# A two-layer encoder trunk on one core: the conditioning dot products of the projection and FFN loops move from TensorE to VectorE

## The chip, the cores and the metric

The kernel runs on one core of a Trainium2 chip. Its time is the device time of one execution, in microseconds (us); of several runs the median is given.

## What is computed

Two layers act on x (256 tokens, width 2048). Before each sublayer x is normalized by rows and modulated by vectors that come from one conditioning vector c. Cut to what matters:

```python
cond = silu(c)                                   # (1, 2048)
for l in range(2):
    mod = (cond @ w_ada[l] + b_ada[l])[:, None]  # w_ada[l]: 2048 x 12288
    sh1, sc1, g1, sh2, sc2, g2 = split(mod, 6)
    z = (rms_norm(x) * (1 + sc1) + sh1) @ w_in[l]
    mix = concat(diff_attention(z), latent_attention(z), spatial_gating(z)) @ w_out[l]
    x = x + g1 * mix
    h = rms_norm(x) * (1 + sc2) + sh2
    a = causal_conv(h @ w_up[l])                 # 3 taps a channel, 2 x 5632 channels
    x = x + g2 * ((silu(a_gate) * a_val) @ w_down[l])
```

All is float32. `cond @ w_ada` reads 201 MB of weights for 24576 results; this is the part that the change touches.

## The kernel before

**Units.** The large products are cut into units of weights, 1 MB each (a raw tile of 128 x 2048). SyncE loads a unit into `raw` (four slots). ScalarE makes its high part `whi` (L1007, in `split_hi`), VectorE its low part `wlo` (L1358, in `split_lo`), each with two slots, and TensorE (L542) does 48 matmuls with a unit: two chunks of 24, each of three products (high by high, high by low, low by high) over eight k. ScalarE may start on unit U when TensorE has done with unit U-2.

**Blocks and rows.** Four units are one block, that is one turn of a loop. The program is a list of rows of blocks (`make_phases`), and for each row each engine has a loop of its own (the first block is written out ahead of the loop in some rows). In layer 0 the rows are: win 6 and win 2 blocks (projection), attention, wout 4, then three times up and down: up 8, down 4, up 8, down 4, up 6, down 4. Layer 1 is alike, with its wout cut into 2 and 2. The units of the third down have 36 matmuls in place of 48.

**The order on VectorE and ScalarE.** In the loop of a block VectorE splits units 2, 3, 4 and 5 counted from the block's first, so always one or two ahead of TensorE. After each split comes the epilogue of one accumulator bank: two taps of the convolution (L1651, L1653) in up, one update of `xT` (L1663) in wout and down. ScalarE does the same with its splits, the first tap (L1250) and, at the end of an up block, the silu (L1256). GpSimd multiplies the two halves of an up block and splits the product (L500, L504, L507; the function is `gated`).

**The conditioning.** Its products are cut into 96 groups of 256 columns. A group comes in four parts of 512 KB, which GpSimd loads into the two slots of `ada` (L487), each when `ada_used` says that the part two before it is done with. On TensorE `ada_part` runs four matmuls a part on 32 columns each, with `condr` (cond, copied to 32 columns), into `B_ADA`; ScalarE copies the group's sums to `ya` (`ada_copy`); `ada_turn` sums their rows and turns them by two matmuls into `B_MOD`; VectorE adds the bias (`mod_add`, L1375). The first 16 groups run in the prologue, 12 in the attention of each layer, and 56 in the other rows, one to a block: all blocks of layer 0, the 8 win blocks of layer 1 and the first 2 of its wout. There a part follows the first chunk of each unit, and the turn the last chunk of the block.

**GpSimd's queue in an up loop** is one line of work: turn i loads parts 0, 1 and 2 of group i, then runs `gated(i - 1)`, then loads part 3. The load of part 2 waits for part 0 of the same group to be used. ScalarE's first tap of block i waits for the product of `gated(i - 1)` (`a_ready`).

Of the kernel before, what the change touches and what calls it, by code (L numbers as in the profile page):

```python
# [28 lines left out]
ALU = mybir.AluOpType  # L29
# [155 lines left out]
def bass_trunk(nc, consts, x, c, positions, w_ada, b_ada, w_in, da_q_gain, da_k_gain, da_lq1, da_lk1,  # L185
# [4 lines left out]
    with ExitStack() as ctx:  # L190
# [67 lines left out]
        T, _ = place("T", 4 * S)  # L258
        ya, _ = place("ya", 256)
        stat, _ = place("stat", 2 * 16)  # L260
        sml, _ = place("sml", 64)
# [21 lines left out]
        unit_done, chunk0_done = sem("unit_done"), sem("chunk0_done")  # L283
        ada_used, mod_turned = sem("ada_used"), sem("mod_turned")
        sub_done, ring_full = sem("sub_done"), sem("ring_full")
# [254 lines left out]
        def _(pe):  # L540
# [54 lines left out]

            def ada_part(g, q, slot, buf, lap):
                if q == 0 and not (isinstance(g, int) and g == 0):

                    pe.wait_ge(ya_ready, g)
                pe.wait_ge(ada_loaded[slot], 16 * lap)  # L600
                for j in range(4):
                    k = 4 * q + j
                    i_ = mm(B_ADA[32 * j:32 * j + 32, 0:256], condr[:, k * 32:(k + 1) * 32],
                            buf[:, slot * 1024 + j * 256:slot * 1024 + (j + 1) * 256], q == 0, q == 3)
                i_.then_inc(ada_used, 1)

            def ada_part_later(g, q):

                ada_part(g, q, q % 2, ada, A_PRO // 2 + 2 * (g - A_PRO) + q // 2 + 1)

            def ada_turn(g):

                pe.wait_ge(ya_ready, g + 1)
                if not (isinstance(g, int) and g == 0):

                    pe.wait_ge(mod_ready, g)
                for v in range(2):
                    i_ = mm(B_MOD[:, v:v + 1], ya[:, v * P:(v + 1) * P], con[:, C_SEL:C_SEL + 1], True, True)
                i_.then_inc(mod_turned, 1)
# [43 lines left out]
            for g in range(A_PRO):  # L663
                for q in range(4):
                    ada_part(g, q, (4 * g + q) % 8, apro, g // 2 + 1)
                    if q == 2 and g >= 1:
                        ada_turn(g - 1)
# [6 lines left out]
            ada_turn(A_PRO - 1)  # L674

            class Fill:


                def __init__(self, g):
                    self.g, self.calls = g, 0  # L680

                def __call__(self):
                    v = self.calls
                    self.calls += 1
                    if v < 10:
                        for q in range(2):
                            ada_part_later(self.g + v // 2, 2 * (v % 2) + q)
                    if v % 2 == 0 and v >= 2:
                        ada_turn(self.g + v // 2 - 1)

# [175 lines left out]

            def heads(l, g):
# [12 lines left out]

                for i in range(15):
                    if i < 12:
                        score(l, i)
                    if i in (4, 6, 8):
                        ms_rows(l, J_O, con[:, C_ROW1:C_ROW1 + 11], 1, only=(i - 4) // 2)
                    if i == 10:
                        spread(0)
                        spread(1)
                    if i == 11:
                        spread(2)  # L890
                    if 2 <= i <= 13:
                        turn_probabilities(l, i - 2)

                    if i < 2 * A_HEADS:
                        for q in range(2):
                            ada_part_later(g + i // 2, 2 * (i % 2) + q)
                    if i % 2 == 0 and i >= 2:
                        ada_turn(g + i // 2 - 1)
                    if 2 <= i <= 13:
                        values(l, i - 2)  # L900
# [22 lines left out]
            for l in range(L):  # L923
# [3 lines left out]
                for row in phases[l]:  # L927
                    kind, p, first, n, u0, b0, g0 = row
                    if kind == "small":
                        attention_inputs(l, u0, b0, Fill(g0))  # L930
                        heads(l, g0 + A_FILL)
                        continue
# [17 lines left out]
                    def body(i, waits):  # L950
                        for b2 in range(2):
# [4 lines left out]
                            for s in range(2):  # L956
                                v = 2 * b2 + s

                                def after_chunk(c_):
                                    if g0 is None:  # L960
                                        return

                                    if c_ == 0:
                                        ada_part_later(g0 + i, v)
                                    elif v == 3:
                                        ada_turn(g0 + i)

# [5 lines left out]
                    if begins and not (kind == "up" and p > 0):  # L973
                        body(0, input_ready)
                        start = 1
                    if start < n:
                        with pe.Fori(start, n) as i:
                            body(i, None)


# [14 lines left out]
        def _(act):  # L995
# [212 lines left out]
            for l in range(L):  # L1208
# [3 lines left out]
                for row in phases[l]:  # L1212
# [10 lines left out]
                    def body(i, ending=False):  # L1223
                        pb = sum(PASS_BLOCKS[:p])
                        pair = l * (FFC // 4) + pb + first + i
                        for b2 in range(2):
                            for c_ in range(2):
                                v = 2 * b2 + 2 + c_
                                if not (ending and b2 == 1):

                                    act.wait_ge(unit_done, d0 + 4 * i + v - 1)
                                    split_hi((u0 + v) % 4, (u0 + v) // 4 + i)
                                if v == 4 and g0 is not None:
                                    ada_copy(g0 + i)
                                if kind not in ("win", "up"):
# [42 lines left out]
        def _(dve):  # L1278
# [91 lines left out]
            def mod_add(g):  # L1370
# [3 lines left out]
                dst = mod[:, bass.ds(2 * at_, 2)]  # L1374
                tt(dst, B_MOD[:, 0:2], cols[:, bass.ds(COL_BADA + 2 * at_, 2)], ALU.add).then_inc(mod_ready, 1)  # L1375

            def t_free(idx):
# [240 lines left out]
            for l in range(L):  # L1618
                if l > 0:
                    trunk(l, J_N1, T_N1, 0)  # L1620
                for row in phases[l]:
# [13 lines left out]
                    def body(i, ending=False):  # L1635
                        n0 = order.n
                        order.plus = links * i
                        for b2 in range(2):
                            for c_ in range(2):
                                v = 2 * b2 + 2 + c_  # L1640
                                if not (ending and b2 == 1):
                                    split_lo(u0 + 4 * i + v, (u0 + v) % 4)
                                if kind == "win":
                                    continue
# [10 lines left out]
                                else:  # L1655
                                    if c_ == 0:
                                        dve.wait_ge(chunk0_done, b0 + 2 * i + b2 + 1)
                                    else:
# [5 lines left out]
                                        acc_free, 1)  # L1664
                        if g0 is not None:
                            mod_add(g0 + i)
                        assert order.n - n0 == links
# [6 lines left out]
                    m = n - ends  # L1674
                    if m > 0:
                        with dve.Fori(0, m) as i:
                            n0 = body(i)
                        order.n = n0 + links * m
                    if ends:
# [49 lines left out]
```

## Time and profile before

| | |
|---|---|
| median of 3 runs | 2923.38 us (2917.65 to 2926.26) |
| span of the profiled execution | 2919.7 us |
| TensorE busy | 2749.6 us, 94% |
| VectorE, ScalarE, GpSimd busy | 46%, 38%, 15% |
| share of TensorE in the chain that ended last | 85% |

The profile is of one execution. Its page gives busy times, the chain of waits that ended last, and groups of instructions; the trace behind it gives each instruction's start, length, and what ended the idle time ahead of it. TensorE's row is the one that a reader would look at first: in the loops it has no gap, and the other engines wait for it.

### The profile page before, as it was taken

To read this page: it belongs to the slowest core of one execution; us is meant where nothing else is said; L and a number is where in the kernel's file an instruction comes from. 1 tells how busy PE (TensorE), PEld (TensorE's weight loads), DVE (VectorE), ACT (ScalarE), POOL (GpSimd) and SP (SyncE) were. 2 spreads that over 40 slices of the span, in tenths; PEclk is the share of its full clock that TensorE was granted. 3 is DMA by queue.
4 is the path that set the end of the run, shared out by engine and by line. 5 is a ranking of instruction groups with operands and counts; after the bars stand their busy time and mean duration, and the time that the engine had idled before them with its cause. 6 is when DMAs were issued, how large, how long until landed. Compare 5 with 4: busy or idle time off the path is not lost.

```text
span 2919.7 us, 55413 instructions
## 1 busy us (share of the span) xinstructions
PE 2749.6 (94%) x22176; PEld 2440.2 (84%) x22176; DVE 1340.7 (46%) x1599; ACT 1119.0 (38%) x1295; POOL 431.8 (15%) x520
## 2 busy tenths in 40 slices
PE   6899887998999999999998998879989999999999
PEld 3499764697999999999987997546989999999998
DVE  1433336345444444444455333363455545554554
ACT  1333343225333333323334333432355534433443
POOL 4211111111221122212211111111001100110110
PEclk8699976799999999999999999877999999999999
DMA  9977653475777777777776775534535555555543
GB/s 321 333 238 237 191 193 119 143 238 173 237 238 238 238 237 240 236 242 233 236 226 194 238 239 185 195 123 159 188 130 172 186 178 183 186 174 187 176 159 126
DMA packets 443877, 595.89 MB, mean 204 GB/s; under 512 B 18124, under 2 KB 391936, under 8 KB 443520
## 3 DMA queue, kind: packets, MB, share of 16 engines
q1 hardware_dynamic: 388080, 392.45, 42.3%
q0 software_dynamic: 55296, 201.35, 20.5%
q8 instruction: 75, 1.23, 0.2%
q10 hardware_dynamic: 400, 0.65, 0.1%
q14 instruction: 26, 0.21, 0.0%
HBM read 592.30 MB, written 2.10 MB: 204 GB/s over the span
## 4 chain that ended last, share of the span: by engine, by line
PE 85%; DMA 7%; DVE 3%; ACT 2%; issue 2%; POOL 1%; POOLq 0%; ACTq 0%; DVEq 0%; SPq 0%
PE bank L542 84%; DMA ada<-in_w_ada_dram 4%; DMA apro<-in_w_ada_dram 1%; DMA raw<-in_w_in_dram 1%; ACT whi L1007 1%; DVE wlo L1358 0%; ACT sq L1074 0%; DVE T L1400 0%; DVE hlo L1405 0%; DMA rows<-in_b_ada_dram 0%; DVE r L1390 0%; PE bank L851 0%; PE bank L574 0%; POOL apro L481 0%; POOL yv L500 0%
## 5 line engine op out<-in xcount | busy, mean ns | idle before, releaser
L1358 DVE TENSOR_TENSOR wlo<-raw,whi 128x2048 fp32r<-128x2048 f32 x374 | 871.3, 2330 | 1223.2 <-ACT whi L1007 1223.2
L1007 ACT ACTIVATE whi<-raw 128x2048 fp32r<-128x2048 f32 (+2 forms) x386 | 725.4, 1881 | 1224.1 <-PE bank L542 1219.5
L542 PE MATMUL bank<-hhi,whi 128*128 128x256 f32 x3872 | 1121.2, 290 | 20.7 <-DVE hlo L1405 15.0
L542 PE MATMUL bank<-hlo,whi 128*128 128x256 f32 x3872 | 1097.7, 284 | 0.0
L542 PE MATMUL bank<-hhi,wlo 128*128 128x256 f32 x3872 | 1096.8, 283 | 0.0
L542 PEld LDWEIGHTS bank<-hhi,whi 128*128 128x128 f32 x3872 | 743.4, 192 | 88.5 <-issue 79.8
L542 PEld LDWEIGHTS bank<-hlo,whi 128*128 128x128 f32 x3872 | 745.3, 192 | 0.0
L542 PEld LDWEIGHTS bank<-hhi,wlo 128*128 128x128 f32 x3872 | 744.6, 192 | 0.0
L542 PE MATMUL bank<-mhi,whi 128*128 128x256 f32 x1920 | 555.5, 289 | 9.5 <-POOL mlo L507 8.4
L542 PE MATMUL bank<-mlo,whi 128*128 128x256 f32 x1920 | 544.9, 284 | 0.0
L542 PE MATMUL bank<-mhi,wlo 128*128 128x256 f32 x1920 | 544.5, 284 | 0.0
L487 POOL DMA_DIRECT2D ada<-in_w_ada_dram x320 | 241.0, 754 | 1598.7 <-PE bank L542 1548.5
L542 PEld LDWEIGHTS bank<-mhi,whi 128*128 128x128 f32 x1920 | 369.6, 192 | 41.7 <-issue 32.3
L542 PEld LDWEIGHTS bank<-mlo,whi 128*128 128x128 f32 x1920 | 370.2, 193 | 0.0
L542 PEld LDWEIGHTS bank<-mhi,wlo 128*128 128x128 f32 x1920 | 369.8, 193 | 0.0
L542 PE MATMUL bank<-ada,condr 128*32 128x256 f32 x2560 | 219.1, 423 | 48.1 <-DMA ada<-in_w_ada_dram 41.1
L500 POOL TENSOR_TENSOR yv<-yv,yg 128x512 f32<-128x512 f32 x44 | 56.9, 1293 | 734.9 <-DVE yv L1653 733.4
L542 PEld LDWEIGHTS bank<-ada,condr 128*32 128x32 f32 x2560 | 56.4, 113 | 115.1 <-DMA ada<-in_w_ada_dram 54.9
L542 PE MATMUL bank<-sq,con 128*128 128x256 f32 (+2 forms) x224 | 69.1, 446 | 39.1 <-ACT sq L1048 28.9
L1007 ACT ACTIVATE ya<-bank 128x256 f32<-128x256 f32 x96 | 36.7, 382 | 152.4 <-PE bank L542 152.4
L542 PEld LDWEIGHTS bank<-sq,con 128*128 128x128 f32 (+2 forms) x224 | 31.1, 164 | 73.0 <-issue 46.8
L542 PEld LDWEIGHTS bank<-con,ya 128*128 128x128 f32 x384 | 61.1, 225 | 26.2 <-issue 22.9
(170 smaller groups left out, 1668.1 us busy)
## 6 DMA issues: line engine op xcount, KB each, us to landing
raw<-in_ffn_w_up_dram SPq DMA_DIRECT2D x176, 1024.0 KB, 5.1
ada<-in_w_ada_dram POOLq DMA_DIRECT2D x320, 512.0 KB, 5.2
raw<-in_w_in_dram SPq DMA_DIRECT2D x64, 1024.0 KB, 7.0
raw<-in_ffn_w_down_dram SPq DMA_DIRECT2D x64, 1024.0 KB, 5.9
apro<-in_w_ada_dram POOLq DMA_DIRECT2D x64, 512.0 KB, 11.0
raw<-in_w_out_dram SPq DMA_DIRECT2D x32, 1024.0 KB, 6.7
raw<-in_ffn_w_down_dram SPq DMA_DIRECT2D x32, 768.0 KB, 4.9
raw<-in_mla_w_uq_dram SPq DMA_DIRECT2D x6, 768.0 KB, 5.7
```

Of the source, the lines that this page charges most:

```text
L487: pool.dma_start(slot_of(ada, q % 2), part_of(l, q, lg * 256)).then_inc(ada_loaded[q % 2], 16)
L500: pool.tensor_tensor(yv[:, 0:512], yv[:, 0:512], yg[:, 0:512], ALU.mult).then_inc(a_ready, 1)
L542: return pe.matmul(out_, lhsT, rhs, start=start, stop=stop, skip_group_check=True)
L1007: return act.activation(out_, in_, ACT.Copy)
L1358: tt(wlo[:, o:o + UNIT], raw[:, v4 * UNIT:(v4 + 1) * UNIT], whi[:, o:o + UNIT].bitcast(F32), ALU.subtract).then_inc(lo_ready, 1)
```

## The change

In the 56 blocks VectorE now forms the products: `dot_part` multiplies a part's four 128 x 256 tiles by one value of cond in each partition and adds them up in a tile `dot`. This takes four instructions a part, 16 a group, each of which waits for the one ahead of it. After a group TensorE only sums `dot` over its 128 rows, by two matmuls with a column of ones (`dot_turn`). `ada_copy` is gone there. The prologue and the attention are as before.

```diff
+            def dot_turn(g):
+
+                pe.wait_ge(ada_used, 4 * g + 4)
+                pe.wait_ge(mod_ready, g)
+                for v in range(2):
+                    i_ = mm(B_MOD[:, v:v + 1], dot[:, v * P:(v + 1) * P], one, True, True)
+                i_.then_inc(mod_turned, 1)
...
-                                    if c_ == 0:
-                                        ada_part_later(g0 + i, v)
-                                    elif v == 3:
-                                        ada_turn(g0 + i)
+                                    if c_ == 1 and v == 1 and not (isinstance(i, int) and i == 0):
+                                        dot_turn(g0 + i - 1)
...
+                    elif g0 is not None:
+                        body(0, None)
+                        start = 1
                     if start < n:
                         with pe.Fori(start, n) as i:
                             body(i, None)
+                    if g0 is not None:
+                        dot_turn(g0 + n - 1)
...
-                                if v == 4 and g0 is not None:
-                                    ada_copy(g0 + i)
...
+            def dot_part(g, q, done):
+
+
+                if q == 0:
+
+                    dve.wait_ge(mod_turned, g)
+                dve.wait_ge(ada_loaded[q % 2], 16 * (A_PRO // 2 + 2 * (g - A_PRO) + q // 2 + 1))
+                for j in range(4):
+                    k = 4 * q + j
+                    w = ada[:, (q % 2) * 1024 + j * 256:(q % 2) * 1024 + (j + 1) * 256]
+                    if k == 0:
+                        i_ = ts(dot[:, 0:256], w, sml[:, 32:33], None, ALU.mult)
+                    else:
+                        i_ = stt(dot[:, 0:256], w, sml[:, 32 + k:33 + k], dot[:, 0:256], ALU.mult, ALU.add)
+                    if j < 3:
+                        i_.then_inc(dot_step, 1)
+                        dve.wait_ge(dot_step, 12 * done + 3 * q + j + 1)
+                    else:
+                        i_.then_inc(ada_used, 1)
+                        dve.wait_ge(ada_used, 4 * g + q + 1)
...
                                 if not (ending and b2 == 1):
                                     split_lo(u0 + 4 * i + v, (u0 + v) % 4)
+                                if g0 is not None:
+                                    dot_part(g0 + i, 2 * b2 + c_, g0 + i - dots_on_pe)
+                                if v == 3 and g0 is not None and not (isinstance(i, int) and i == 0):
+                                    mod_add(g0 + i - 1)
...
-                        if g0 is not None:
-                            mod_add(g0 + i)
...
+                    if peeled:
+                        mod_add(g0 + n - 1)
```

On VectorE, the start of a block in an up loop, before; `hi_ready` is ScalarE's split, `tap_ready` its tap:

```order
L1358 TENSOR_TENSOR wlo<-raw,whi 128x2048 [waits hi_ready]
L1648 REGISTER_ALU
L1651 ISA [waits tap_ready]
L1651 SCALAR_TENSOR_TENSOR yg<-bank,cols,yg 128x255
L342 REGISTER_ALU
L1653 ISA [waits dve_order]
L1653 SCALAR_TENSOR_TENSOR yg<-bank,cols,yg 128x254
L1356 REGISTER_ALU
L1358 TENSOR_TENSOR wlo<-raw,whi 128x2048 [waits hi_ready]
```

and in the changed kernel:

```order
L1369 TENSOR_TENSOR wlo<-raw,whi 128x2048 [waits hi_ready]
L1393 REGISTER_ALU
L1394 ISA [waits mod_turned]
L1399 TENSOR_SCALAR dot<-ada,sml 128x256 [waits ada_loaded0]
L1404 ISA
L1401 SCALAR_TENSOR_TENSOR dot<-ada,sml,dot 128x256 [waits dot_step]
L1404 REGISTER_ALU
L1401 SCALAR_TENSOR_TENSOR dot<-ada,sml,dot 128x256 [waits dot_step]
L1404 REGISTER_ALU
L1401 SCALAR_TENSOR_TENSOR dot<-ada,sml,dot 128x256 [waits dot_step]
L1407 ISA
L1684 REGISTER_ALU [waits ada_used]
```

Four products now stand between the split and the taps that follow it. The waits on `dot_step` are carried by the products themselves, the wait for ScalarE's tap by an instruction of its own, as before.

On TensorE, the end of the first win row, where the loop is left, before:

```order
L542 MATMUL bank<-hhi,wlo 128x256
L613 REGISTER_ALU
L542 MATMUL bank<-con,ya 128x1 [waits mod_ready,ya_ready]
L542 MATMUL bank<-con,ya 128x1
L977 REGISTER_ALU
L977 COMPARE_AND_BRANCH
```

and in the changed kernel:

```order
L543 MATMUL bank<-hhi,wlo 128x256
L988 REGISTER_ALU
L988 COMPARE_AND_BRANCH
L543 MATMUL bank<-con,dot 128x1 [waits mod_ready,ada_used]
L543 MATMUL bank<-con,dot 128x1
L543 MATMUL bank<-hhi,whi 128x256 [waits acc_free,lo_ready]
```

The turn of a row's last group stands behind the loop and ahead of the next row's first unit; it waits for that group's four parts (`ada_used`).

On GpSimd the up loop is unchanged; in the changed kernel it reads:

```order
L487 REGISTER_ALU
L488 ISA [waits ada_used]
L488 DMA ada<-in_w_ada_dram 128x4x256
L500 ISA [waits silu_done]
L501 ISA
L501 TENSOR_TENSOR yv<-yv,yg 128x512 [waits acc_free]
L505 ISA [waits a_ready]
L505 COPY mhi<-yv 128x512
```

Nothing has moved here; what has moved is who raises `ada_used`: VectorE, after the split of unit 2, where it was TensorE in the middle of unit 0.

## Rows read from the trace of the kernel before

**Rows 1.** The page: its head, and the shares of the chain by engine.
```profile
span 2919.7 us, 55413 instructions
...
PE 85%; DMA 7%; DVE 3%; ACT 2%; issue 2%; POOL 1%; POOLq 0%; ACTq 0%; DVEq 0%; SPq 0%
```
**Rows 2.** Timeline, ScalarE, up block with a group: start, length, instruction, idle before.
```profile
1009.40 1.92 ACT L1007 ACTIVATE whi<-raw 128x2048 fp32r<-128x2048 f32 x1 [5.12 <-PE bank L542]
...
1025.82 0.39 ACT L1007 ACTIVATE ya<-bank 128x256 f32<-128x256 f32 x1 [1.56 <-PE bank L542]
...
1035.89 1.92 ACT L1007 ACTIVATE whi<-raw 128x2048 fp32r<-128x2048 f32 x1 [4.15 <-PE bank L542]
1038.96 0.57 ACT L1250 ACTIVATE yg<-bank,cols 128x256 f32<-128x256 f32 x1 [1.16 <-PE bank L542]
```
**Rows 3.** Timeline, ScalarE, one up block of layer 1, without a group.
```profile
2425.29 1.91 ACT L1007 ACTIVATE whi<-raw 128x2048 fp32r<-128x2048 f32 x1 [2.03 <-PE bank L542]
...
2448.33 1.91 ACT L1007 ACTIVATE whi<-raw 128x2048 fp32r<-128x2048 f32 x1 [2.03 <-PE bank L542]
```
**Rows 4.** Timeline, TensorE, on both sides of one part.
```profile
700.54 0.28 PE L542 MATMUL bank<-hhi,wlo 128*128 128x256 f32 x1
...
701.54 0.28 PE L542 MATMUL bank<-hlo,whi 128*128 128x256 f32 x1
```
**Rows 5.** Timeline, VectorE, a split and its two taps in an up block.
```profile
1011.35 2.29 DVE L1358 TENSOR_TENSOR wlo<-raw,whi 128x2048 fp32r<-128x2048 f32 x1 [4.29 <-ACT whi L1007]
1013.56 0.48 DVE L1651 SCALAR_TENSOR_TENSOR yg<-bank,cols,yg 128x255 f32<-128x255 f32 x1
1014.19 0.48 DVE L1653 SCALAR_TENSOR_TENSOR yg<-bank,cols,yg 128x254 f32<-128x254 f32 x1 [0.15 <-DVE yg L1651]
```
**Rows 6.** Timeline, VectorE, two instructions that follow on each other, and one alone.
```profile
88.75 0.56 DVE L1342 SCALAR_TENSOR_TENSOR dist<-dist 128x384 f32<-128x384 f32 x1
89.34 0.50 DVE L1344 TENSOR_SCALAR ang<-ang,con 128x256 f32<-128x256 f32 x1
...
682.29 0.48 DVE L1400 SCALAR_TENSOR_TENSOR T<-xT,sml,r 128x256 f32<-128x256 f32 x1
```
**Rows 7.** Timeline, GpSimd, in the block of rows 2.
```profile
1026.44 0.75 POOL L487 DMA_DIRECT2D ada<-in_w_ada_dram  x1 [5.72 <-PE bank L542]
1033.37 0.75 POOL L487 DMA_DIRECT2D ada<-in_w_ada_dram  x1 [6.18 <-PE bank L542]
1034.20 1.28 POOL L500 TENSOR_TENSOR yv<-yv,yg 128x512 f32<-128x512 f32 x1
```
**Rows 8.** Timeline at two row ends: layer 0's win, then its wout.
```profile
341.77 0.39 PE L542 MATMUL bank<-hhi,whi 128*128 128x256 f32 x1 [1.93 <-ACT z L1007]
...
664.39 0.50 PE L542 MATMUL bank<-con,ya 128*128 128x1 f32 x4
666.94 5.51 PE L542 MATMUL bank<-sq,con 128*128 128x256 f32 x17 [2.06 <-ACT sq L1074]
...
664.59 1.91 ACT L1007 ACTIVATE whi<-raw 128x2048 fp32r<-128x2048 f32 x1 [2.65 <-PE bank L542]
```
**Rows 9.** Timeline, ScalarE, one block of the third down of layer 0.
```profile
1498.38 1.91 ACT L1007 ACTIVATE whi<-raw 128x2048 fp32r<-128x2048 f32 x1 [3.16 <-PE bank L542]
...
1519.10 1.91 ACT L1007 ACTIVATE whi<-raw 128x2048 fp32r<-128x2048 f32 x1 [3.16 <-PE bank L542]
```
**Rows 10.** Timeline, ScalarE, third down of layer 1: two units on, TensorE waiting once.
```profile
2859.74 1.92 ACT L1007 ACTIVATE whi<-raw 128x2048 fp32r<-128x2048 f32 x1 [2.94 <-PE bank L542]
...
2868.82 1.92 ACT L1007 ACTIVATE whi<-raw 128x2048 fp32r<-128x2048 f32 x1 [2.93 <-PE bank L542]
```
**Rows 11.** TensorE after two gaps; stretches: us, busy, granted clock, DMA share, GB/s.
```profile
1487.90 0.45 PE L542 MATMUL bank<-mhi,whi 128*128 128x256 f32 x1 [1.86 <-POOL mlo L507]
...
1488.00:1491.00 3.00, 3.00 (x17) 0.51 0.53 168
...
2840.35 0.58 PE L542 MATMUL bank<-mhi,whi 128*128 128x256 f32 x1 [4.71 <-POOL mlo L507]
...
2840.00:2845.00 5.00, 4.65 (x22) 0.50 0.45 147
```

More of the change, by code:

```diff
@@ L259, in bass_trunk @@
         ya, _ = place("ya", 256)
+        dot, _ = place("dot", 256)
         stat, _ = place("stat", 2 * 16)
@@ L283, in bass_trunk @@
         unit_done, chunk0_done = sem("unit_done"), sem("chunk0_done")
-        ada_used, mod_turned = sem("ada_used"), sem("mod_turned")
+        ada_used, mod_turned, dot_step = sem("ada_used"), sem("mod_turned"), sem("dot_step")
         sub_done, ring_full = sem("sub_done"), sem("ring_full")
@@ L593, in turn_vectors, with ada_part @@
                     last.then_inc(pro_full, 1)
-            def ada_part(g, q, slot, buf, lap):
-                if q == 0 and not (isinstance(g, int) and g == 0):
-                    pe.wait_ge(ya_ready, g)
+            def ada_part(g, q, slot, buf, lap, copies):
+                if q == 0 and copies > 0:
+                    pe.wait_ge(ya_ready, copies)
                 pe.wait_ge(ada_loaded[slot], 16 * lap)
@@ L605, in ada_part, with ada_part_later, ada_turn @@
                 i_.then_inc(ada_used, 1)
[L607 to L613, printed above, removed]
+            def ada_part_later(g, q, copies):
+                ada_part(g, q, q % 2, ada, A_PRO // 2 + 2 * (g - A_PRO) + q // 2 + 1, copies)
+            def dot_turn(g):
[4 more added lines that the diff above has]
+                i_.then_inc(mod_turned, 1)
+            def ada_turn(g, copies):
+                pe.wait_ge(ya_ready, copies + 1)
                 if not (isinstance(g, int) and g == 0):
@@ L664, in _ @@
                 for q in range(4):
-                    ada_part(g, q, (4 * g + q) % 8, apro, g // 2 + 1)
+                    ada_part(g, q, (4 * g + q) % 8, apro, g // 2 + 1, g)
                     if q == 2 and g >= 1:
-                        ada_turn(g - 1)
+                        ada_turn(g - 1, g - 1)
                 if g == 2:
@@ L673, in _, with __init__ @@
                     turn_vectors()
-            ada_turn(A_PRO - 1)
+            ada_turn(A_PRO - 1, A_PRO - 1)
             class Fill:
-                def __init__(self, g):
-                    self.g, self.calls = g, 0
+                def __init__(self, g, copies):
+                    self.g, self.copies, self.calls = g, copies, 0
                 def __call__(self):
@@ L686, in __call__ @@
                         for q in range(2):
-                            ada_part_later(self.g + v // 2, 2 * (v % 2) + q)
+                            ada_part_later(self.g + v // 2, 2 * (v % 2) + q, self.copies + v // 2)
                     if v % 2 == 0 and v >= 2:
-                        ada_turn(self.g + v // 2 - 1)
+                        ada_turn(self.g + v // 2 - 1, self.copies + v // 2 - 1)
             def ring(l, e, b0):
@@ L865, in values, with heads @@
                     o_full, 1)
-            def heads(l, g):
+            def heads(l, g, copies):
                 def spread(v):
@@ L895, in heads @@
                         for q in range(2):
-                            ada_part_later(g + i // 2, 2 * (i % 2) + q)
+                            ada_part_later(g + i // 2, 2 * (i % 2) + q, copies + i // 2)
                     if i % 2 == 0 and i >= 2:
-                        ada_turn(g + i // 2 - 1)
+                        ada_turn(g + i // 2 - 1, copies + i // 2 - 1)
                     if 2 <= i <= 13:
@@ L929, in _ @@
                     if kind == "small":
-                        attention_inputs(l, u0, b0, Fill(g0))
-                        heads(l, g0 + A_FILL)
+                        copies = A_PRO + A_ATT * l
+                        attention_inputs(l, u0, b0, Fill(g0, copies))
+                        heads(l, g0 + A_FILL, copies + A_FILL)
                         continue
@@ L1636, in body @@
                         n0 = order.n
-                        order.plus = links * i
+                        order.plus = 0 if isinstance(i, int) else links * (i - peeled)
                         for b2 in range(2):
@@ L1674, in _ @@
                     m = n - ends
-                    if m > 0:
-                        with dve.Fori(0, m) as i:
+                    dots_on_pe = A_PRO + A_ATT * (l + (kind != "win"))
+                    peeled = int(g0 is not None)
+                    if peeled:
+                        body(0)
+                    if m > peeled:
+                        with dve.Fori(peeled, m) as i:
                             n0 = body(i)
-                        order.n = n0 + links * m
+                        order.n = n0 + links * (m - peeled)
+                    if peeled:
+                        mod_add(g0 + n - 1)
                     if ends:
```

## The prediction

> **What bounds the kernel now.** The page first: TensorE carries 85% of the chain that ended last [rows 1], so the question is what a block costs on TensorE, and whether anything else can reach it. Next the timeline of ScalarE, whose splits of weights mark the ends of TensorE's units. An up block with a group takes 1035.89 - 1009.40 = 26.49 us [rows 2], one without 2448.33 - 2425.29 = 23.04 us [rows 3], which is 192 matmuls at 0.12 us. In both ScalarE waits for TensorE. Of the 3.45 us between them the parts carry most: between the two matmuls around a part lie 1.00 us [rows 4], where two of 0.12 us would be 0.24, so a part costs 0.76 and four cost 3.04. The turn keeps the other 0.41.
>
> Then the cover. After unit U-2 ScalarE splits for 1.92 us, VectorE for 2.29 [rows 2, 5], 4.24 us with the handover; a unit of 48 matmuls takes 5.76. So unit U has 1.5 us to spare, and what delays either split by more stops TensorE. The times below are those of one profiled execution, span 2919.7 us [rows 1]; it lies 3.7 us under the median, and I carry changes over one to one.
>
> **1. The products leave TensorE.** 56 groups x 3.04 = -170.2 us. ScalarE's copy goes too; it was hidden in idle time [rows 2]. A block with its turn is then 23.45 us.
>
> **2. What a part costs on VectorE.** A 128x256 product with a scalar from SBUF takes 0.48 us [rows 6]. One that waits for the instruction ahead starts 0.03 us after its end (89.34 against 88.75 + 0.56 [rows 6]); one that doesn't wait starts 0.08 before (1013.56 against 1011.35 + 2.29 [rows 5]). No row has this wait with a value from a register. The nearest, between two taps, is carried by an instruction of its own and leaves 0.15 us [rows 5]; here the product itself carries it, so I take 0.03 and keep 0.15 as the other end. A part: 3 x 0.51 + 0.48 = 2.01 us. With the split (2.21 to the start of the next), 0.15 ahead of the tap, and the taps' pair (0.63 + 0.48 - 0.08 = 1.03), VectorE needs 5.40 us a unit in up, 21.7 a block, below 23.45. By sums it fits.
>
> **3. The order in up loops, where it doesn't fit.** GpSimd loads part 2 of group i before it runs the product of block i-1, and that load waits until part 0 is used. Today TensorE uses it in mid unit 0; the product starts at 1034.20, and ScalarE's tap, which needs it, comes at 1038.96 for other reasons [rows 2, 7]. Now VectorE uses part 0 after the split of unit 2. Let that split start at s. Part 0 ends at s + 4.22. From there: 0.62 until the load is issued (1026.44 - 1025.82, both released by the same part [rows 2, 7]), load 0.75, to the product 0.08, product 1.28 [rows 7], wake of ScalarE 0.10 (estimated), tap 0.57 less 0.10 overlap, ScalarE's split of unit 3 1.92, handover 0.03: 5.25 us. VectorE starts the split of unit 3 at T = s + 9.47.
>
> Then TensorE starts unit 3 at T + 2.29. A wait of TensorE adds 0.52 us: two units of the last down take 9.08 from ScalarE to ScalarE [rows 10], of which 1.92 + 0.03 + 2.29 and 36 x 0.12 = 4.32 are work. Unit 3 is done at T + 8.57, the next at T + 14.33, the next block's split of unit 2 starts 1.95 later, at T + 16.28 (VectorE is free at T + 16.27). A block so takes 16.28 + 9.47 = 25.75 us: 2.30 more than TensorE needs, and only 0.74 less than before. This holds for all blocks of an up row in layer 0 but the first, 7 + 7 + 5 = 19: **+43.7 us**.
>
> **4. The ends of rows.** The turn of a row's last group stands on TensorE ahead of the next row's first unit, and waits for part 3, which VectorE forms only after the split of a unit that ScalarE may begin when the row's last unit is done. Now the turn starts at 664.39, ScalarE's split at 664.59 [rows 8]. In the changed kernel the turn waits 0.20 + 1.95 + 4.22 + 0.04 = 6.4 us. There are 12 such rows:
> - five with TensorE busy on both sides (first win row of each layer, two downs, wout in layer 1): 32.0;
> - two ahead of attention, where 1.93 us are idle already [rows 8]: 8.9;
> - wout of layer 0, ahead of a norm, 2.06 idle already [rows 8], and one square of the norm is done meanwhile (0.7, estimated): 3.6;
> - three ups: VectorE is late (the split starts at T + 10.87), so 6.7 each, less the 1.86 idle that it replaces at one [rows 11]: 18.4;
> - the third down, VectorE late as well, ahead of a norm: 4.2.
>
> Together **+67.1 us**.
>
> **5. The third down.** Its units need 4.32 us on TensorE, but on VectorE 2.21 + 2.01 + 0.15 + 0.40 = 4.77, a block 19.3 with the addition of the bias. Before it was 20.72 [rows 9], so it gains 1.42 in place of 3.04: 4 x 1.62 = **+6.5**. In win, wout and the other downs VectorE stays under 5.76 a unit and is hidden.
>
> **6. The clock.** After a gap of 4.71 us TensorE ran at a granted 0.50 (1.2 GHz) for at least 5 us, after one of 1.86 us for some 3 [rows 11]; and I take the loss behind a gap of some 2 us to be rarer than behind one of 4. Half the time at half clock is lost. For a row end I take 2.5 us, for 8 ends inside loops 20.0, less 1.7 that one of them pays today, and 1.7 for each of the two ahead of attention: 21.7. For the 19 stops of step 3, each some 1.9 us long, I take 0.25 us. Together **+26.5**; the ends are 10 and 85.
>
> **Sum.** -170.2 + 43.7 + 67.1 + 6.5 + 26.5 = -26.4, a span of 2893.3 and a median of **2897 us**, 0.9% faster. A sixth of the work saved is left.
>
> **The rivals.**
> *VectorE is slower than taken* (0.13). If each product's wait leaves 0.15 us as between the taps, a part takes 2.34 us. Then VectorE sets the up block: T + 17.3 in place of T + 16.28, and 0.33 more ahead of T, 1.3 x 19 = 25; 12 row ends 4; third down 5; about 35 in all: 2932 us, at the edge of no change. For it: those two taps are the only chained pair in a loop. Against it: the order shows no instruction between the products that waits.
>
> *The clock falls at every stop* (0.12), the slower case. If each of the 19 stops costs not 0.25 but 3.4 us (6.8 us at half clock, two stretches as behind the gap of 1.86) and the eight row ends 3.4, that is 60 + 7 more: 2964 us. It becomes slower than before by 0.3% once a stop costs 2.1 us. For it: the gap of 1.86 us had its drop [rows 11], and these stops are as long. Against it: in a block TensorE then runs over 20 us without a gap, and in the next 20 the clock has time to rise; how often so short a gap lowers it the rows leave open.
>
> *The wait costs VectorE nothing* (0.05). Then each product starts 0.11 us earlier, a part takes 1.68, and steps 3, 4 and 5 shrink by 19 x 0.33 + 12 x 0.33 + 5 = 15: 2882 us. The rows speak against it, with 0.03 after an end beside 0.08 before one [rows 5, 6]. The Trainium skill, page "VectorE: DVE Perf Modes", section "The DRAIN you can't avoid", states it: the next instruction starts only once the pipe is empty, and a semaphore after each costs nothing extra. By that rule the sum would be 2882 us, by the rows 2897.
>
> *The up loops keep their cover* (0.06): GpSimd's order does not bind, since I misread who waits. Without step 3 and its clock, 43.7 + 4.8 less: 2849 us.
>
> *The full gain* (0.04): neither step 3 nor step 4 binds: 2923.4 - 170.2 + 6.5 = 2760 us. For it stands only that busy shares leave VectorE room.
>
> **How the numbers follow.** My own case has 0.60. With step 6 at 10 or 85 it runs from 2881 to 2956, and I take 2875 to 2930 as its own. Some 0.3% (8.8 us) is what a measurement of this kernel can tell from no change, so the bounds are 2914.6 and 2932.2. Faster: 0.50 of my case, 0.05, 0.06 and 0.04: 0.65. Same: 0.10 of my case and 0.04 of the slow VectorE: 0.14. Slower: 0.09 and 0.12: 0.21. The range leaves out the full gain and most of the clock's case: 2848 to 2945.
>
> **What would show it.** Step 1: no matmul with `ada` after the prologue outside attention, and win blocks of 23.45 us. Step 2: four products in 2.0 us. Step 3: up blocks of layer 0 of 25.7 us, TensorE idle before unit 3, GpSimd's product after a load that VectorE released, and ScalarE's tap right behind the product. Step 4: twelve gaps of 6.4 to 7 us ahead of the matmuls with `dot`. Step 5: blocks of 19.3 us. Step 6: the granted clock behind each gap. The sum is wrong first if up blocks differ from 25.7 (each 0.5 us is 9.5 us), or if the clock behind row ends stays full.

## The result and the profile after

The changed kernel takes 2967.34 us (median of 4 runs, 2966.11 to 2968.79), the kernel before 2921.56 (median of 4, 2917.65 to 2926.26). The ratio is 1.0159, with a 95% interval of 1.0144 to 1.0174: 1.6% slower, where 0.9% faster was forecast, and outside the forecast range of 2848 to 2945. The profiled execution has a span of 2966.3 us; before it was 2919.7 [rows 1]. The span so grew by 46.6 us and was forecast to shrink by 26.4; 73.0 us are to be found.

The page of the changed kernel: its head, TensorE's line, and the shares of the chain that ended last.

```profile
span 2966.3 us, 52970 instructions
...
PE 2649.4 (89%) x20384; PEld 2453.4 (83%) x20384; DVE 1762.2 (59%) x2495; ACT 1097.6 (37%) x1239; POOL 431.0 (15%) x520
...
PE 75%; DVE 8%; DMA 7%; ACT 4%; issue 4%; POOL 2%; ACTq 0%; POOLq 0%; DVEq 0%; SPq 0%
```

TensorE's share of the chain fell from 85% [rows 1] to 75%; VectorE's rose from 3% to 8%, ScalarE's from 2% to 4%. VectorE is busy for 59% of the span only: over the whole it doesn't lack time, others wait for its next result.

The list of waits of TensorE, changed kernel: us in total, times, longest.

```profile
PE bank L543 <- DVE wlo L1369: 82.0, 36, 4.0
PE bank L543 <- DVE dot L1401: 76.9, 12, 7.6
```

Before, neither is among its ten longest. The second line is the twelve row ends of step 4. The first is step 3 for the most part: 19 stops of 3.9 to 4.0 us. By rows of layer 0 (first to last matmul, from the timeline; the forecast is the time before, less 3.04 us a group, and in the ups 2.30 + 0.25 us more for each of 7, 7 and 5 stops; a row that follows the end of an up or a down also has the 2.5 us that step 6 gives to the clock behind that end):

| Row | before | after | forecast |
|---|---|---|---|
| first up | 214.7 | 234.2 | 208.2 |
| second up | 211.7 | 229.9 | 205.2, with the clock of a row end 207.7 |
| third up | 158.7 | 174.6 | 153.2, with the clock of a row end 155.7 |
| first down | 105.7 | 95.3 | 93.5, with the clock of a row end 96.0 |

The three ups miss by 26.0 + 22.2 + 18.9 = 67.1 us, most of the error. Two ends ahead of a norm carry nearly all of the rest: from the last matmul of wout to the first of the first up 17.18 us became 23.94 (644.01 to 667.95), where 3.6 more were forecast, and from the third down to layer 1 they became 24.74 (1613.66 to 1638.40), where 4.2 more were; together 6.5 us too much. The other differences cancel to less than 1 us; the largest is layer 1's attention, 6 us shorter, which the change doesn't touch. The first down shows a row in which all is hidden, ScalarE's timeline, changed kernel:

```profile
952.01 1.91 ACT L1020 ACTIVATE whi<-raw 128x2048 fp32r<-128x2048 f32 x1 [4.28 <-PE bank L543]
...
975.48 1.92 ACT L1020 ACTIVATE whi<-raw 128x2048 fp32r<-128x2048 f32 x1 [4.28 <-PE bank L543]
```

A block takes 23.47 us, forecast 23.45: step 1 holds. Now one up block. VectorE's timeline, then GpSimd's and ScalarE's, the rows that answer to [rows 2, 5, 7]:

```profile
1044.52 2.29 DVE L1369 TENSOR_TENSOR wlo<-raw,whi 128x2048 fp32r<-128x2048 f32 x1 [0.57 <-ACT whi L1020]
1048.71 0.35 DVE L1399 TENSOR_SCALAR dot<-ada,sml 128x256 f32<-128x256 f32 x1 [1.89 <-PE bank L543]
1049.10 1.52 DVE L1401 SCALAR_TENSOR_TENSOR dot<-ada,sml,dot 128x256 f32<-128x256 f32 x3
...
1055.97 2.29 DVE L1369 TENSOR_TENSOR wlo<-raw,whi 128x2048 fp32r<-128x2048 f32 x1 [0.53 <-ACT whi L1020]
...
1051.27 0.75 POOL L488 DMA_DIRECT2D ada<-in_w_ada_dram  x1 [6.94 <-DVE dot L1401]
1052.03 1.30 POOL L501 TENSOR_TENSOR yv<-yv,yg 128x512 f32<-128x512 f32 x1
...
1053.57 0.56 ACT L1261 ACTIVATE yg<-bank,cols 128x256 f32<-128x256 f32 x1 [9.08 <-POOL yv L501]
1054.04 1.90 ACT L1020 ACTIVATE whi<-raw 128x2048 fp32r<-128x2048 f32 x1
```

The order forecast in step 3 is all there: part, load, product of GpSimd, tap, ScalarE's split, VectorE's split. From the end of part 0 (1050.62) to VectorE's split (1055.97) are 5.35 us, forecast 5.25. But part 0 doesn't stand behind the split. VectorE is free at 1046.81 and idles for 1.89 us, for TensorE. TensorE's timeline and, behind it, stretches of 4 us (busy, matmuls, granted clock, DMA share, GB/s):

```profile
1048.05 0.50 PE L543 MATMUL bank<-con,dot 128*128 128x1 f32 x4
1058.31 0.58 PE L543 MATMUL bank<-hhi,whi 128*128 128x256 f32 x1 [3.91 <-DVE wlo L1369]
...
1056.00:1060.00 4.00, 1.69 (x8) 0.55 0.07 16
1060.00:1064.00 4.00, 4.00 (x23) 0.60 0.92 290
1064.00:1068.00 4.00, 4.00 (x36) 1.00 0.83 281
```

What VectorE waits for is the turn of the group before, at 1048.05, at the end of TensorE's unit 1: the first product overwrites `dot`, which the turn reads. So TensorE stops for 3.91 us, not for the some 1.9 forecast, and after the stop its granted clock is 0.60, half speed for most of 4 us (23 matmuls instead of 36). The 16 distances between neighbouring stops in the three ups sum to 473.3 us, 29.58 a block.

The chain of waits over one block closes the loop (start, length, what; the other pieces are left out):

```profile
1058.31 20.03 PE bank L543 x148
...
1078.50 0.36 DVE dot L1399
...
1081.83 1.31 POOL yv L501
...
1083.84 1.91 ACT whi L1020
...
1085.77 2.30 DVE wlo L1369
...
1088.12 4.00 PE bank L543 x17
```

TensorE reaches its turn, VectorE's first product follows that, and everything up to TensorE's next unit 3 follows the product.

### The profile page after: what moved, and what is told of

Its sections match the earlier page's. It is cut to its first block, busy times and chain, and to the rows that moved or that the text cites. A ratio compares the mean times of both kernels' runs of the same rounds, so it can differ in the third digit from the quotient of the medians.

```text
span 2966.3 us, 52970 instructions
## 1 busy us (share of the span) xinstructions
PE 2649.4 (89%) x20384; PEld 2453.4 (83%) x20384; DVE 1762.2 (59%) x2495; ACT 1097.6 (37%) x1239; POOL 431.0 (15%) x520
## 4 chain that ended last, share of the span: by engine, by line
PE 75%; DVE 8%; DMA 7%; ACT 4%; issue 4%; POOL 2%; ACTq 0%; POOLq 0%; DVEq 0%; SPq 0%
PE bank L543 74%; DMA ada<-in_w_ada_dram 4%; DVE wlo L1369 3%; ACT whi L1020 3%; DVE dot L1401 2%; DMA apro<-in_w_ada_dram 1%; POOL yv L501 1%; DMA raw<-in_w_in_dram 1%; DVE T L1432 1%; DVE hlo L1437 1%; POOL ada L488 0%; DMA rows<-in_b_ada_dram 0%; DVE r L1422 0%; ACT sq L1087 0%; DVE dot L1399 0%
## 5 line engine op out<-in xcount | busy, mean ns | idle before, releaser
L543 PE MATMUL bank<-hlo,whi 128*128 128x256 f32 x3872 | 1120.5, 289 | 0.0
L543 PE MATMUL bank<-hhi,wlo 128*128 128x256 f32 x3872 | 1119.1, 289 | 0.0
L543 PEld LDWEIGHTS bank<-hhi,whi 128*128 128x128 f32 x3872 | 769.5, 199 | 101.3 <-DVE wlo L1369 81.4
L543 PEld LDWEIGHTS bank<-hlo,whi 128*128 128x128 f32 x3872 | 770.5, 199 | 0.0
L543 PEld LDWEIGHTS bank<-hhi,wlo 128*128 128x128 f32 x3872 | 768.8, 199 | 0.0
L1401 DVE SCALAR_TENSOR_TENSOR dot<-ada,sml,dot 128x256 f32<-128x256 f32 x840 | 406.2, 484 | 24.0
L543 PE MATMUL bank<-ada,condr 128*32 128x256 f32 x768 | 74.9, 488 | 50.6 <-DMA ada<-in_w_ada_dram 43.4
L1261 ACT ACTIVATE yg<-bank,cols 128x256 f32<-128x256 f32 x88 | 49.0, 557 | 191.9 <-POOL yv L501 173.3
L543 PE MATMUL bank<-con,dot 128*128 128x1 f32 x224 | 34.1, 256 | 76.9 <-DVE dot L1401 76.9
L543 PEld LDWEIGHTS bank<-con,dot 128*128 128x128 f32 x224 | 34.4, 219 | 79.3 <-DVE dot L1401 79.3
```

The lines of the kernel that those rows point to most:

```text
L543: return pe.matmul(out_, lhsT, rhs, start=start, stop=stop, skip_group_check=True)
L1261: act.activation(ch(yv if b2 else yg, c_), bank[2 * b2 + c_][:, 0:S], ACT.Identity, bias=cols[:, bass.ds(cc + 3 * FFC, 1)], scale=cols[:, ...
L1401: i_ = stt(dot[:, 0:256], w, sml[:, 32 + k:33 + k], dot[:, 0:256], ALU.mult, ALU.add)
```

## The experiments

The theory after the result: the extra time is the stop of the up loops, its length set by the wait for the turn (`mod_turned`) and by GpSimd's order, and half clock behind each stop. The rivals: VectorE lacks time; the row ends cost it; the clock alone does. Unless said otherwise an edit is made on the changed kernel, and a ratio is to the kernel before, measured anew beside it (medians 2922.0 to 2924.5), with its 95% interval.

**The sum apart.** The products add up in a tile that only VectorE uses; the 16th alone writes `dot` and waits.

```diff
-                if q == 0:
-                    dve.wait_ge(mod_turned, g)
...
-                        i_ = ts(dot[:, 0:256], w, sml[:, 32:33], None, ALU.mult)
+                        i_ = ts(rt_tmp[:, 0:256], w, sml[:, 32:33], None, ALU.mult)
+                    elif k < 15:
+                        i_ = stt(rt_tmp[:, 0:256], w, sml[:, 32 + k:33 + k], rt_tmp[:, 0:256], ALU.mult, ALU.add)
                     else:
-                        i_ = stt(dot[:, 0:256], w, sml[:, 32 + k:33 + k], dot[:, 0:256], ALU.mult, ALU.add)
+                        dve.wait_ge(mod_turned, g)
+                        i_ = stt(dot[:, 0:256], w, sml[:, 32 + k:33 + k], rt_tmp[:, 0:256], ALU.mult, ALU.add)
```

> The changed kernel, but the products of a group add up in a tile of their own, and only the last of the sixteen writes `dot`; so the wait for TensorE's turn of the group before stands ahead of the last product, not of the first. Theory (the first product's wait for that turn, queued ahead of GpSimd's product, makes the up blocks long): the gap ahead of unit 3 falls from 4.0 to about 2 us, an up block from 29.5 to 26 to 27 us, the median from 2967 to 2910 (2890 to 2930). Rival (only GpSimd's order matters, and VectorE's wait lies beside it): no change, 2967.

Measured: 2927.31 us, ratio 1.0008 (0.9986 to 1.003), 40 us less than the changed kernel; in the expected range, near its upper end, and no different from before. VectorE's and TensorE's timeline, this kernel:

```profile
1111.01 2.29 DVE L1369 TENSOR_TENSOR wlo<-raw,whi 128x2048 fp32r<-128x2048 f32 x1 [0.24 <-ACT whi L1020]
1113.22 0.35 DVE L1396 TENSOR_SCALAR rt_tmp<-ada,sml 128x256 f32<-128x256 f32 x1
...
1122.84 0.39 PE L543 MATMUL bank<-hhi,whi 128*128 128x256 f32 x1 [1.96 <-DVE wlo L1369]
```

The product starts with the split's end and the stop is 1.96 us, as the some 1.9 of the forecast. From split to split VectorE takes 9.49 us (1111.01 to 1120.50), forecast 9.47. So the wait for the turn was what the first half of step 3 had left out. The block is 27.2 us, though, not 25.75 (expected here: 26 to 27); the rest is the clock and VectorE's second half of the block, below.

**GpSimd's product ahead of the load of part 2.**

```diff
                             if ada_row:
-                                group(i, range(3))
+                                group(i, range(2))
                             gated(i - 1)
                             if ada_row:
-                                group(i, (3,))
+                                group(i, (2, 3))
```

> The changed kernel, but GpSimd loads part 2 of a group after `gated` of the block before, not ahead of it; VectorE's wait for the turn stays. Theory (the stop needs both, the late use of part 0 and the product queued behind it): no gap ahead of unit 3, up blocks of 23.5 us, 19 x 6.0 us less, about 2852 (2840 to 2870). Rival (the wait for the turn alone makes the stop, since the split of unit 3 stands behind it on VectorE): up blocks stay above 27 us and the median above 2920.

Measured: 2885.37 us, ratio 0.9883 (0.9843 to 0.9924): 82 us gained, so the chain does go through GpSimd's order. But it is 15 us above the expected range: blocks take 25.2 us, and a stop of up to 1.40 us remained where none was expected. Both edits together:

> Both edits together: the wait for the turn ahead of the last product, and `gated` ahead of the load of part 2. Theory: as with the second edit alone, 2850, since without the queue on GpSimd the wait for the turn fits beside TensorE's unit 2. Rival (each edit takes away its own part of the stop): at least 15 us less than with the second edit alone.

Measured: 2876.52 us, ratio 0.9849 (0.981 to 0.9888), with blocks of 24.7 us and stops of 0.8 to 0.9. That is neither of the two cases: 26 us above what was expected, and only 9 below the second edit alone. With GpSimd's order put right the wait for the turn costs 0.5 us a block, so the 3.9 us of stop are no sum of two shares: one edit alone takes away half of them, the other 2.5 us, both together 3.1. What remains is in the timelines of VectorE and GpSimd, both edits:

```profile
1113.32 2.29 DVE L1369 TENSOR_TENSOR wlo<-raw,whi 128x2048 fp32r<-128x2048 f32 x1
1115.53 1.37 DVE L1396 TENSOR_SCALAR rt_tmp<-ada,sml 128x256 f32<-128x256 f32 x1
1116.93 2.87 DVE L1398 SCALAR_TENSOR_TENSOR rt_tmp<-ada,sml,rt_tmp 128x256 f32<-128x256 f32 x3
...
1113.38 3.37 POOL L501 TENSOR_TENSOR yv<-yv,yg 128x512 f32<-128x512 f32 x1
```

GpSimd's product, started 0.06 us after VectorE's split, takes 3.37 us instead of 1.30 and ends 1.14 us after it; VectorE's first product takes 1.37 instead of 0.35 and ends 0.15 after GpSimd's. Each seems to hold the other up. To see whether it does, GpSimd's three steps of a block were cut from 512 columns to 2:

> The changed kernel with both edits of e3_both, and GpSimd's three steps of an up block on 2 columns in place of 512; so the product of the two FFN halves is left out for all but 2 columns. Theory (in e3_both GpSimd's product and VectorE's split hold each other up, 3.37 us in place of 1.30, and after it VectorE's first product 1.37 in place of 0.35): VectorE's products keep 0.35 and 0.51 us, the gap of 0.87 us ahead of unit 3 is gone, up blocks of layer 0 take 23.5 us in place of 24.6. Rival (the gap comes from VectorE's sum of work, 5.5 us a unit): the gap stays above 0.6 us.

Measured: 2849.87 us (one run, span 2848.2). First a stretch of TensorE in the second up (us, busy, matmuls, granted clock, DMA share, GB/s), then VectorE's and GpSimd's timeline, this kernel:

```profile
1040.00:1140.00 100.00, 100.00 (x837) 1.00 0.80 268
```

```profile
1092.59 2.29 DVE L1369 TENSOR_TENSOR wlo<-raw,whi 128x2048 fp32r<-128x2048 f32 x1 [0.24 <-ACT whi L1020]
1094.80 0.35 DVE L1396 TENSOR_SCALAR rt_tmp<-ada,sml 128x256 f32<-128x256 f32 x1
1095.18 1.52 DVE L1398 SCALAR_TENSOR_TENSOR rt_tmp<-ada,sml,rt_tmp 128x256 f32<-128x256 f32 x3
...
1092.80 2.13 POOL L505 CAST mhi<-yv 128x2 f32 x1 [0.18 <-POOL yv L501]
```

TensorE doesn't stop at all in this row, and the blocks take 23.47 us, as expected. VectorE's products are back at 0.35 and 1.52 us. And a conversion of two columns, begun during VectorE's split, ends 0.05 us after it: it isn't slowed but held. The Trainium skill, page "SBUF — State Buffer", section "Who interferes with whom", states it: a VectorE instruction with two inputs from SBUF and a GpSimd instruction that reads SBUF exclude each other, and the first has the port for its whole length. These rows agree, 2.13 us for two columns. How much of the 0.88 us of stop the exclusion is worth this run doesn't separate, since on two columns the product itself takes 0.19 us in place of 1.30.

**GpSimd's order in the kernel before.** The same edit as in the second experiment, on the kernel before.

> The kernel before, with GpSimd's load of part 2 behind `gated`, the second edit alone. Theory (before the change this order was hidden): no difference, 2915 to 2930, up blocks of 26.5 us. Rival (GpSimd's order cost the kernel before as well): at least 10 us faster.

Measured: 2921.57 us, ratio 1.0013 (0.9995 to 1.0032). The order costs nothing there; it only costs once part 0 is used late.

**The row ends alone.** Only the products of part 3 go ahead of the split beside them.

```diff
+                                if g0 is not None and v == 5:
+                                    dot_part(g0 + i, 2 * b2 + c_, g0 + i - dots_on_pe)
                                 if not (ending and b2 == 1):
                                     split_lo(u0 + 4 * i + v, (u0 + v) % 4)
-                                if g0 is not None:
+                                if g0 is not None and not (v == 5):
                                     dot_part(g0 + i, 2 * b2 + c_, g0 + i - dots_on_pe)
```

> The changed kernel, but the products of part 3 of each group stand ahead of the split that they stood behind; nothing else moves. Theory (the turn of a row's last group waits for that split, a gap of 6.3 us and a low clock behind it): the twelve gaps fall to about 3 us, 12 x 3.3 = 40 us less and up to 15 us of clock, 2920 (2905 to 2935). Rival (the row ends cost little, since later waits take up what they leave): above 2950.

Measured: 2956.55 us, ratio 1.0129 (1.0102 to 1.0156), a gain of 11 us where 47 was expected: a miss. TensorE's waits, this kernel:

```profile
PE bank L543 <- DVE wlo L1369: 95.6, 50, 4.1
PE bank L543 <- DVE dot L1401: 41.6, 12, 5.9
```

The profiled execution is the fastest of the four (2946.57 us), so its trace accounts for 21 us of gain, not 11. The row ends give 76.9 - 41.6 = 35 us, but the split now stands behind four products and comes late in every block that has no slack: the waits for it rise by 13.6 us in 14 more places, and the blocks of the third down go from 20.25 to 23.9 us (1573.92 to 1594.17, and 1562.49 to 1586.40 in this kernel), that row from 79.7 to 91.0. The median is where the rival had it (above 2950), but the ends aren't cheap: the edit pays for them elsewhere. The row ends are real, and not what the 73 us are.

**All three**, with each part's products, not only the last's, ahead of the split; and the same with GpSimd's order left as it is. (The conditions are constants: the products always stand ahead of the split.)

```diff
+                                if g0 is not None and True:
+                                    dot_part(g0 + i, 2 * b2 + c_, g0 + i - dots_on_pe)
                                 if not (ending and b2 == 1):
                                     split_lo(u0 + 4 * i + v, (u0 + v) % 4)
-                                if g0 is not None:
+                                if g0 is not None and not (True):
                                     dot_part(g0 + i, 2 * b2 + c_, g0 + i - dots_on_pe)
```

> Both edits, and each part's products ahead of the split that they stood behind, so that a row's last turn no longer waits for the split of a unit that can't begin before the row is done. Theory (row ends cost 6.3 us and a drop of the clock each): the twelve gaps shrink from 6.3 to 1 to 2 us, the clock stays full behind most, 12 x 5 and some 20 us less than with both edits alone, about 2775 (2760 to 2800). Rival (VectorE has no room: the products now delay the splits themselves): new gaps ahead of units in the loops, and no more than 30 us gained.

> As e5_all, but with GpSimd's order as in the changed kernel (load of part 2 ahead of `gated`). Theory (the order on GpSimd costs only because part 0 is used late; with the products ahead of the split it is used about 2.2 us earlier): up blocks within 0.7 us of the 24.2 of e5_all, median 2780 to 2795. Rival (the queue costs as long as VectorE uses part 0 at all in unit 1): a gap of 1.5 us or more ahead of unit 3, median above 2805.

Measured: 2779.65 us, ratio 0.9521 (0.9481 to 0.9561), and 2780.86 us, ratio 0.9513 (0.947 to 0.9557), both in their expected ranges. With the products before the split, part 0 is used early enough that GpSimd's order doesn't matter, as in the kernel before. TensorE's waits, all three:

```profile
PE bank L543 <- DVE dot L1401: 14.9, 12, 2.6
PE bank L543 <- DVE wlo L1369: 10.8, 21, 1.5
```

159 us of waits have become 26. This is a kernel that beats both: 4.8% under the kernel before. VectorE has time for the same products in it, so its sum of work isn't what made the change slower. It isn't far away either: in the third down it sets the block, and in the ups a part of it (below).

**The clock.** 30 matmuls that nothing reads, some 3.76 us, fill the stop of each up block of layer 0; the chain stays as it is.

```diff
+                                    if kind == "up" and c_ == 1 and v == 2 and not isinstance(i, int):
+                                        for _ in range(30):
+                                            mm(bank[6][:, 0:S], hhi[:, 0:P], ch(hhi, 1), True, True)
```

> The changed kernel with 30 more matmuls of hhi by hhi (3.6 us at 0.12), into a bank that is free there, behind unit 2 in each up block of layer 0 but a row's first; nobody reads their result. They stand in the gap of 3.9 us ahead of unit 3. Theory (behind each gap the granted clock falls to half and costs some 2 us of an up block's 29.5): full clock in these rows, blocks of 27.5 us, 19 x 2.0 = 38 us less, median 2929 (2920 to 2940). Rival (the low clock lies beside waits and costs nothing): 2967 or more.

Measured: 2941.15 us, ratio 1.0063 (1.004 to 1.0087): 26 us gained by adding work, one us above the expected range. The block is 27.77 us, where 27.5 was expected, at full clock. The three ups are 34 us shorter in the trace; 5.8 us of that are lost again ahead of the first up, where nothing was filled, and 3 at the ends of the ups. The kernel is still slower than before, so the clock alone isn't the cause. The same with 15 matmuls on the kernel with the sum apart:

> The kernel of e1_sum_apart with 15 such matmuls (1.8 us) at the same place, in its gap of 2.0 us. Theory: full clock, up blocks of 25.8 us in place of 27.2, as the walk through rows of the kernel before gave them, 19 x 1.4 = 27 us less than e1_sum_apart, some 2900 (2890 to 2908). Rival (the walk was short of a term and the clock costs nothing there): 2920 or more.

Measured: 2911.89 us, ratio 0.9962 (0.9942 to 0.9981), 4 us above the expected range, with blocks of 26.40 us, where 25.8 was expected. VectorE's timeline, this kernel, the splits of unit 3 and of the next block's unit 2:

```profile
1109.04 2.29 DVE L1372 TENSOR_TENSOR wlo<-raw,whi 128x2048 fp32r<-128x2048 f32 x1 [0.53 <-ACT whi L1023]
...
1113.56 0.16 DVE L1389 TENSOR_TENSOR mod<-bank,cols 128x2 f32 x1 [0.26 <-DVE rt_tmp L1401]
...
1125.95 2.29 DVE L1372 TENSOR_TENSOR wlo<-raw,whi 128x2048 fp32r<-128x2048 f32 x1
```

Between the two lie 16.91 us, forecast 16.28, and VectorE waits for no other engine: at full clock it sets this half of the block. Its units take 5.5 to 5.6 us instead of 5.40, with 0.24 us ahead of the tap where 0.15 was taken, and the one with the addition of a finished turn takes 5.78. The kernel of the run before has the same 16.91 (1105.97 to 1122.88).

At which stop the clock falls is seen in the granted clock behind the stop that ends at 1122.8 us: first the sum apart (1.96 us), then GpSimd's product first (1.40 us), its stop and the stretches. Columns as above; 0.50 is 1.2 GHz, 1.00 is 2.4.

```profile
1124.00:1126.00 2.00, 2.00 (x11) 0.50 0.99 309
1126.00:1128.00 2.00, 2.00 (x14) 0.71 1.08 350
```

```profile
1122.76 0.39 PE L543 MATMUL bank<-hhi,whi 128*128 128x256 f32 x1 [1.40 <-DVE wlo L1369]
...
1124.00:1126.00 2.00, 2.00 (x19) 1.00 0.96 299
1126.00:1128.00 2.00, 2.00 (x19) 1.00 1.10 369
```

11 and 14 matmuls in 2 us against 19 and 19. The stop of 1.96 us has its price, the one of 1.40 has none. With the sum apart the blocks are 27.2 us against 26.4 with filling. The kernel with the sum apart also has its own control. Behind 17 of its 19 stops the clock fell, behind the first stop of the first and of the second up it did not:

```profile
1042.03 0.39 PE L543 MATMUL bank<-hhi,whi 128*128 128x256 f32 x1 [1.95 <-DVE wlo L1369]
...
1044.00:1046.00 2.00, 2.00 (x19) 1.00 1.06 377
```

From this stop to the next are 26.45 us (1042.03 to 1068.48), from a stop with the drop to the next 27.2, as with and without filling. Why these two were spared the runs don't show.

## Why the prediction was wrong

**Step 1 held**: 23.47 us a block where all is hidden. The matmuls with `ada` are gone from the rows' loops.

**Step 2 held.** Four products take 2.04 us, forecast 2.01, at a pitch of 0.51. The rival with 0.15 behind each product is out, and so is the one in which the wait costs nothing. By the rule of the Trainium skill cited there (page "VectorE: DVE Perf Modes", section "The DRAIN you can't avoid") a part would take 1.68 us, and the rows decide against it.

**Step 3 failed, first of all in its line "Part 0 ends at s + 4.22".** The excerpt of VectorE's order showed `L1394 ISA [waits mod_turned]` ahead of the first product, and the diff showed the turn at `c_ == 1 and v == 1`. Both stand ahead of the prediction and neither was put into the walk. Part 0 is so bound to the end of TensorE's unit 1; it ended at s + 6.10 (1050.62 against 1044.52). A block at full clock is 27.77 us (measured with filling) instead of 25.75: 19 x 2.02 = 38 us. Of the 2.02 the wait is 27.77 - 26.40 = 1.37, 26 us in all. The other 0.65, 12 us, is the second half of the walk: VectorE was to be free at T + 16.27, 0.01 ahead of need, and was free at T + 16.91, in part for the addition of the finished turn (0.26), which the walk doesn't name there. With the wait taken away the first half was right, 9.49 us against 9.47.

**Step 4 held in its waits**: 76.9 us in twelve, 6.4 each; at the ends ahead of busy units 6.28, at the third down 7.61. Its total was 6.5 us low at the two ends ahead of a norm, where it took off the idle time that was there before and one square: the distances grew by 6.8 and 7.6 us.

**Step 5 came out right as a sum, in part by luck.** Its blocks take 20.26 us instead of 19.3, but the first only 18.65 (1544.50 to 1563.15). The whole row went from 86.3 to 79.7 us, 6.6 less, where steps 4 to 6 together give 6.7 less. VectorE still sets the block; ahead of the update of `xT` it has 0.30 to 0.35 us of idle time where 0.15 was taken, and the addition of a finished turn takes its own wait.

**Step 6 failed for the 19 stops.** 0.25 us each was taken "rarer than behind one of 4", and the stop was as long as 4. Each of the 19 lowers the clock, and some for longer: the distances are 28.9 to 29.2 us or 29.8 to 30.4. They average 29.58 against 27.77 at full clock: 1.81 us each, 19 x (1.81 - 0.25) = 30 us. Even with the stop at its forecast length the loss is there, 27.2 against 26.4, 0.8 us each where 0.25 was taken. For the row ends the term was about right; stretches behind the one that ends at 908.48, changed kernel:

```profile
908.00:912.00 4.00, 3.52 (x16) 0.50 0.96 326
912.00:916.00 4.00, 4.00 (x32) 0.87 0.17 57
```

Half of 3.5 us and 0.13 of 4 us are 2.3 us, forecast 2.5.

Together 26 + 12 + 30 = 68 us, against the 67.1 by which the three ups miss; with the 6.5 of step 4 these are the 73 that were sought, to within 2. The shares depend on what is taken away first: with the wait gone and the clock left as it falls a block is 2.4 us shorter (29.58 to 27.2), with the clock put right first the wait is worth 1.37. The rival "the clock falls at every stop" named 2964 us; its time is close to the result, but for half of it the cause is another, since it had the clock at 3.4 us a stop and no wait for the turn. The chances had no case in which the walk of step 3 was incomplete, although its length was worked out and each 0.5 us of it was known to be worth 9.5.

## What to carry to other kernels

When work moves to another engine, list every wait that it carries, its buffer's reader too, and place each of them on the time line of one block before the walk starts; a result that is read by the other engine needs either a second buffer or a private sum. Put the new work ahead of the long instruction beside it, if whoever waits for the work is further down a chain and the long one has slack. A stop that comes back every block costs its length and, behind 36 of the 38 of some 2 us and of 4 us here, the clock as well.

## What the runs showed of the hardware

- Stops of TensorE of some 2 us in blocks of 27 lowered the granted clock to 0.50 behind 17 of 19; those of 1.40 in blocks of 25 didn't, nor did those of 0.88. The stops of 3.9 us did so behind all 19. Filling a stop of 3.9 us with useless matmuls gained 26 us.
- VectorE's split (two inputs from SBUF) and GpSimd's instructions exclude each other: 3.37 us for a product of 1.30, 2.13 us for a conversion of two columns, and then 1.37 us on VectorE for a product of 0.35. In the changed kernel this doesn't show, since there VectorE is idle while GpSimd multiplies.
- A product with one input from SBUF besides its scalar takes 0.35 us, one that also adds takes 0.48 us.
